# Block-banded first attention group in a TensorE-bound encoder layer: scores per block of 32 positions, one tile per projection unit

## What is computed

```python
ATT_GROUPS = ((128, 1), (512, 4), (2048, 16))   # window, dilation; 8 heads of 64 each
# query at t attends to keys t + j*dil, |j| <= window/(2*dil): group 0 to |offset| <= 64
s = where(mask, q . k, -inf);  m = max(s);  p = exp(s - m);  l = sum(p);  acc = p @ v
# over the three groups: w = exp(m_g - max m);  att = sum(w*acc) / sum(w*l)
```

## Time and profile before

| | |
|---|---|
| median of 3 runs | 2489.22 µs |
| profiled execution, span from first to last instruction | 2486.3 µs |
| PE busy | 2460.4 µs (99%) |
| DVE busy / ACT busy | 1648.8 µs (66%) / 1385.6 µs (56%) |
| granted TensorE clock, mean | 0.996 |

### The profile page before, as it was taken

The page is one execution under the profiler, slowest core; times in us unless marked ns, Lnnn a source line. Parts: engine busy times, 40 slices in busy tenths (PEclk is TensorE's granted clock), DMA queues, the critical chain, the costliest instruction groups (busy, mean ns, idle before and its releaser), DMA issues.

```text
span 2486.3 us, 36774 instructions
## 1 busy us (share of the span) xinstructions
PE 2460.4 (99%) x12848; PEld 2096.6 (84%) x12848; DVE 1648.8 (66%) x2070; ACT 1385.6 (56%) x1542; POOL 323.1 (13%) x287
## 2 busy tenths in 40 slices
PE   8999999999999999999999999999999999999998
PEld 7898989788898989897887688888888888888886
DVE  5454545453544545554434788888888888888887
ACT  4434344432434444445333677777777777777776
POOL 1313122100013122220001100000000000000000
PEclk9999999999999999999999999999999999999999
DMA  4212121122712121112234999999999999999998
GB/s 173 94 41 86 51 93 47 64 85 93 271 54 84 52 93 57 70 53 75 78 145 158 361 386 395 376 399 382 391 383 387 379 386 385 379 389 390 387 383 305
DMA packets 133489, 550.59 MB, mean 221 GB/s; under 512 B 9392, under 2 KB 10032, under 8 KB 125488
## 3 DMA queue, kind: packets, MB, share of 16 engines
q1 hardware_dynamic: 126368, 524.03, 55.4%
q0 software_dynamic: 7056, 25.69, 3.4%
HBM read 528.72 MB, written 20.97 MB: 221 GB/s over the span
## 4 chain that ended last, share of the span: by engine, by line
PE 98%; DVE 1%; DMA 0%; ACT 0%; issue 0%; POOL 0%; SPq 0%; DVEq 0%; ACTq 0%; POOLq 0%
PE bank L1260 42%; PE bank L925 20%; PE bank L970 12%; PE bank L902 7%; PE bank L945 4%; PE bank L986 3%; PE bank L1093 2%; PE bank L1306 2%; PE bank L1054 1%; PE bank L1021 1%; PE bank L1074 1%; PE bank L1034 1%; PE bank L1059 1%; PE bank L1151 1%; PE bank L1109 0%; PE bank L1005 0%
## 5 line engine op out<-in xcount | busy, mean ns | idle before, releaser
L2304 DVE TENSOR_TENSOR m_lo<-m_raw,m_hi 128x2048 fp32r<-128x2048 f32 x380 | 867.4, 2290 | 121.0 <-ACT m_hi L1717 117.6
L1717 ACT ACTIVATE m_hi<-m_raw 128x2048 fp32r<-128x2048 f32 x382 | 733.5, 1921 | 259.9 <-PE bank L1260 256.7
L925 PE MATMUL bank<-w_hi,h_hi 128*128 128x384 f32 (+1 forms) x1024 | 340.9, 333 | 1.7 <-DVE h_lo L2147 0.9
L925 PE MATMUL bank<-w_hi,h_lo 128*128 128x384 f32 (+1 forms) x1024 | 329.9, 322 | 0.0
L925 PE MATMUL bank<-w_lo,h_hi 128*128 128x384 f32 (+1 forms) x1024 | 329.5, 322 | 0.0
L1260 PE MATMUL bank<-m_hi,xs_hi 128*128 128x512 f32 x1032 | 321.0, 392 | 0.0
L1260 PE MATMUL bank<-m_hi,xs_lo 128*128 128x512 f32 x1032 | 317.9, 389 | 0.0
L1260 PE MATMUL bank<-m_lo,xs_hi 128*128 128x512 f32 x1032 | 317.8, 389 | 0.0
L1854 DVE TENSOR_TENSOR w_lo<-w_raw,w_hi 128x1152 fp32r<-128x1152 f32 (+4 forms) x110 | 140.9, 1282 | 212.5 <-ACT w_hi L1380 212.5
L1260 PEld LDWEIGHTS bank<-m_lo,xs_hi 128*128 128x128 f32 x1032 | 193.8, 188 | 40.4
L1260 PEld LDWEIGHTS bank<-m_hi,xs_lo 128*128 128x128 f32 x1032 | 193.8, 188 | 40.3
(11 more groups left out here) (257 smaller groups left out, 3829.9 us busy)
## 6 DMA issues: line engine op xcount, KB each, us to landing
m_raw<-in_w_exp_gate SPq DMA_DIRECT2D x128, 1024.0 KB, 9.3
m_raw<-in_w_exp_up SPq DMA_DIRECT2D x128, 1024.0 KB, 7.0
m_raw<-in_w_exp_down SPq DMA_DIRECT2D x128, 1024.0 KB, 7.6
w_raw<-in_w_b SPq DMA_DIRECT2D x22, 1536.0 KB, 6.7
w_raw<-in_w_a SPq DMA_DIRECT2D x24, 1024.0 KB, 5.1
w_raw<-in_w_c SPq DMA_DIRECT2D x24, 1024.0 KB, 4.7
w_raw<-in_w_d SPq DMA_DIRECT2D x8, 1024.0 KB, 6.0
xt<-in_x SPq DMA_DIRECT2D x8, 512.0 KB, 8.8
```

Of the source, the lines that this page charges most:

```text
L925: last = pe.matmul(ps_proj[:, proj.slot, 0:cols], a[:, c, tokens], v[:, c, :], start=c == n == 0, stop=c == chunks - 1 and n == 2)
L1717: act.activation(m_hi[slot.slot][:, :, :], m_raw[raw.slot][:, :, :], ACT.Copy)\
L2304: dve.tensor_tensor(m_lo[slot.slot][:, :, :], m_raw[raw.slot][:, :, :], m_hi[slot.slot][:, :, :].bitcast(F32), ALU.subtract)\
```

## The change

The three words `S`, `D` become one `S i` for both, `I` is new, and `T`, `U` transpose four blocks each:

```diff
-    order = "P S0 P D0 P P T0 S1 P U0 D1 P P T1 S2 P U1 D2 P P T2 S3 P U2 D3 P"
+    order = "P S0 P S1 P S2 P S3 P P I P P T0 P U0 T1 P U1 T2 P U2 T3 P"
...
-    extra = {0: (("T", 3),), 1: (("U", 3),), 2: (("V",), ("G",)), 3: (("K", 0), ("K", 1)),
+    extra = {0: (("U", 3),), 1: (("V",),), 2: (("G",),), 3: (("K", 0), ("K", 1)),
```

Queries of group 0 are now held by blocks of 32 positions per residue (`by_block`: a tile is 4 residues x 32), and such a tile meets a window of 64 positions x 4 residues, 256 keys (`window_keys`), in place of 512:

```diff
-                            last = pe.matmul(ps_sc[:, a, :], q[head_rows(a), natural(r)], k[head_rows(a), :],
-                                             start=n == 0, stop=n == 2)
+                            pe.matmul(ps_sc[:, a, 0:2 * P], q[head_rows(a), natural(i)], window_keys(k[head_rows(a), :], i),
+                                      start=n == 0, stop=n == 2)
```

```diff
+                elif what == "I":
+
+                    pe.wait_ge(s_same, 1)
+                    all_read(pe, s_sc_free, sc)
+                    pe.wait_ge(s_spread, t["swap"].n(1))
+                    pe.matmul(ps_sc[:, 0, 0:P], same[:, :], spread.rearrange("p (g k s c) -> p (g k s c)"),
+                              start=True, stop=True).then_inc(s_swapped, 1)
...
+                dve.wait_ge(s_exp, t["score"].n())
+                for side in range(2):
+                    own = stats[:, 0, :, 1 - side, :, :].rearrange("p k i a -> p k (i a)")
+                    last = dve.tensor_tensor(spread[:, :, :, side, :], own.unsqueeze(1).to_broadcast([P, NT, 2, 8]),
...
+                dve.wait_ge(s_swapped, t["swap"].n())
...
+                for i in range(NT):
+                    for side, scores in enumerate((near, wide)):
+                        for a in range(2):
+                            last = dve.tensor_scalar(scores[:, i, a, :], scores[:, i, a, :],
+                                                     factor[:, side, i, a:a + 1], None, ALU.mult)
```

`V` has 32 matmuls of 128 columns; the 8 of 512 columns (group 0) are gone. Their values must lie as the windows do, so SP writes `v_a[0]` to memory, waits, and reads it back shifted, between two weight loads:

```diff
-                            pe.matmul(ps_out[head_rows(a), a, :], v_a[0][:, r, head_rows(a)], prob_t[:, a, r, :],
-                                      start=r == 0, stop=False)
+                    for i in range(NT):
+                        for c in range(2):
+                            rows = window(i) // (BLOCK // 2) + 2 * c
+                            for a in range(2):
+                                last = pe.matmul(block_rows(ps_out[head_rows(a), a, :], i), v_shifted[:, rows, head_rows(a)],
+                                                 near[:, i, a, natural(c)], start=False, stop=i == NT - 1 and c == 1)
...
+                sp.wait_ge(s_out, START + t["out"].n())
+                sp.dma_start(v_kept, v_a[0][:, :, :]).then_inc(s_kept, 16)
+                sp.wait_ge(s_kept, t["swap"].n() * 16 + 16)
+                for r in range(RES):
+                    sp.dma_start(v_shifted[BLOCK * r:BLOCK * (r + 1), :, :], kept_rows(r)).then_inc(s_shifted, 16)
```

More of the change, by code:

```diff
@@ L57 @@
 HALVES = ((0, 4), (4, 8))
-PER_HEAD = {"w": 6, "piece": 18, "proj": 20, "first": 1, "pair": 4, "turned": 4, "tr": 26, "sc": 20, "out": 6, "turn": 16, "rope": 16, "ret": 1,
-            "score": 8, "step": 8, "link": 11, "cut": 1}
+PER_HEAD = {"w": 6, "piece": 18, "proj": 20, "first": 1, "pair": 4, "turned": 4, "tr": 22, "sc": 12, "out": 6, "turn": 16, "rope": 16, "ret": 1,
+            "score": 4, "step": 8, "link": 10, "cut": 1, "swap": 1}
 PER_COL = {"w": 4, "piece": 5, "half": 1, "proj": 4 * COLS, "mix": COLS, "hi": COLS}
@@ L578, in _ @@
         def _(sp):
-            t = {"w": Tally(2)}
+            t = some("w", "proj", "out", "swap")
             w = t["w"]
@@ L883, in _ @@
         def _(pe):
-            t = some("w", "proj", "tr", "sc", "out", "rope", "ret", "step", "half", "turned", "cut")
+            t = some("w", "proj", "tr", "sc", "out", "rope", "ret", "step", "half", "turned", "cut", "swap")
             w, proj, tr, sc, outs = t["w"], t["proj"], t["tr"], t["sc"], t["out"]
@@ L1368, in _ @@
         def _(act):
-            t = some("w", "proj", "tr", "sc", "out", "turn", "ret", "score", "mix", "hi", "first", "turned")
+            t = some("w", "proj", "tr", "sc", "out", "turn", "ret", "score", "mix", "hi", "first", "turned", "swap")
             w, proj, tr, sc, outs = t["w"], t["proj"], t["tr"], t["sc"], t["out"]
@@ new lines, in attention_step @@
+                    for side, scores in enumerate((near, wide)):
+                        for a in range(2):
+                            last = act.activation(scores[:, i, a, :], scores[:, i, a, :], ACT.Exp,
+                                                  bias=stats[:, 0, 0, side, i, a:a + 1], scale=DH ** -0.5,
+                                                  accum_out=stats[:, 0, 1, side, i, a:a + 1])
+                    last.then_inc(s_exp, 1)
+                    score.k += 1
+                elif what == "I":
+                    t["swap"].k += 1
+                    act.wait_ge(s_gap, t["swap"].n())
+                    act.activation(share[:, :, :], gap[:, :, :], ACT.Exp).then_inc(s_share, 1)
+                elif what == "T":
+                    act.wait_ge(s_tr, tr.n(1))
+                    act.activation(near[:, arg[0], :, :], ps_tr[:, tr.slot, :].rearrange("p (a n) -> p a n", a=2),
+                                   ACT.Copy).then_inc(s_tr_free[tr.slot], 1)
+                    tr.k += 1
```

260 lines of the change are left out of this document (153 added, 107 removed).

## The result

The changed kernel takes 2504.0 us (median of 4 runs, 2501.9 to 2505.1) against 2488.9 (2486.6 to 2489.6) before, in runs on the same chip: ratio 1.0063, 95% interval 1.0049 to 1.0077. It is slower by 15 us, where I forecast 2463, with 0.89 on faster. The profiled execution has a span of 2500.1 us (2486.3 before).

What follows compares the result with a forecast made beforehand. PE, busy 99% of the span, was taken as the bound: 8 x 3.9 = 31.2 us gained, 5.2 waited, 26.0 net, so span 2460.3 and median 2463 us; range of 8 in 10: 2450 to 2481.

Steps and rivals of the forecast that it cites:

- `I`: Product of 128 columns behind DVE's spread in the head part: 0.2 us of PE waiting per pair, no slack left.
- `S3`: Score products of tile 3 in the head part: no PE wait forecast for the tiles' scores.
- `K`: Third score tile of retention in the tail: PE waits 0.6 us, six times, +3.6 us in all, because `G` starts later.
- PE's own work: PE's instructions in a head pair: 3.9 us less a pair, 31.2 us over 8 pairs.
- The `S` term: Score products, 256-column pairs at 0.18 us instead of 0.23: 12 pairs by 0.05, -0.6 us a pair (0 to -1.4).
- `T` and `U`: Transposes on PE at 0.10 us each, from 48 to 32 a pair: -1.6 us.
- two small spreads (24.3): DVE's last steps before `I`, after `rqk_lo` at 23.85, done at 24.3; PE is ready at 24.4.
- The exponential: ACT's four accumulating activations of 256 columns per tile, 0.37 us each, in a chain step of 4.85 us.
- rival 1: Softmax chain's step about 0.6 us longer, `I` reached 1.8 us late per pair: +14, 2478 us; chance 0.20.
- rival 3: Chain bounds the head part at `I`, PE waits about 5.9 us a pair: 2509 us; break-even 3.5 us; chance 0.07.
- SP's queue: First later load of retention weights, behind `shift_values`, goes about 292, lands about 298.9: hidden with 3.5 us to spare.
- `T0`: First transposes, 5.7 us after `I`; small steps and first two scalings end about 3.5 us after it: 2.2 us spare.

Runs made afterwards that it cites:

- The last kernel: Changed kernel with the second unit's split early, spread ahead of rqk_lo, turn ahead of split, POOL's differences behind the spread, transposes one unit later: 2451.0 us.
- e1: Changed kernel with POOL's two weight differences that fell beside the spread waiting until the product `I` is done: 2479.8 us.
- e4: Changed kernel with the two spreads put ahead of rqk_lo in DVE's queue, POOL's work left in its place: 2465.9 us.
- f4: Changed kernel with early split, spread ahead of rqk_lo, turn ahead of the split, and retention decays `G` one unit earlier: 2455.0 us.
- f2: Changed kernel with the retention turn ahead of the third of the weight split at each unit of the head part: 2464.2 us.
- g1: Changed kernel with whole early split, spread ahead of rqk_lo, turn ahead of split, POOL's differences behind the spread, `G` ahead of its unit's third split: 2475.2 us.

## Why the prediction was wrong

The account, in profiled spans: 2486.3 before, 2500.1 after. The waits of `I`, `S3` and `K` are 42.3 us and the clock costs 15.2, so PE's own work fell by 42.3 + 15.2 - 13.8 = 43.7. The last kernel says nearly the same from the other side: 2449.6 = 2486.3 + 4.8 of waits - 41.5. Against the forecast span of 2460.3 that is 39.8 us too long: 33.8 more at `I`, 4.5 at `S3`, 15.2 of clock, less 1.2 at `K` and less 12.5 of PE's own work.

- **PE's own work: right in kind, priced too low.** 31.2 forecast, 41 to 44 measured. The `S` term was mis-sized: a pair at 0.12 us gives 12 x 0.11 = 1.3 us in place of 0.6, and the eight short products with it take 0.53 and not 0.64. Four transposes take 0.35, so `T` and `U` give 1.9 and not 1.6. The Trainium skill's rule that I weighed ("TensorE: Matmul & The Clock Gate", section "LDWEIGHTS (loading the stationary operand)") gives the time of one load, 107 ns for 128 columns. That the two loads of a pair follow each other, which would hold it at 0.21, was my step, and the 0.12 measured decides against it for these loads of 64 rows. This error helped the kernel but also brought PE to `I` sooner: at 210.95, behind 0.54 of waiting at `S3`, where my times, counted from DVE's start on tile 0 at 191.85, put it at 211.25; so 0.8 us sooner.
- **The step that failed: "two small spreads (24.3)".** I gave them 0.45 us, the price of steps that run alone, and did not ask what POOL does meanwhile. Two instructions took 3.18 us: 2.7 of the 4.4 us. e1 (POOL moved, the spreads as they were) and e4 (the spreads moved, POOL as it was) show the cause from both sides. The Trainium skill, "SBUF — State Buffer", section "Who interferes with whom", says that VectorE and GpSimd share one pair of SBUF ports, which is an exclusive lock, and that a VectorE instruction with two SBUF inputs contends with a GpSimd instruction that reads SBUF, `tensor_reduce` never, `tensor_scalar` if it enters a 2-port mode. The trace agrees, down to the reduction that is not held (0.29 us in e4) and the `TENSOR_SCALAR` that is (0.84 in f4); in which mode that one ran no trace here shows. An estimate by that page: each spread lasts until one of POOL's differences ends, two of them the 3.57 us of POOL's row.
- **The exponential: 0.49 us, not 0.37.** This is a second mis-sized term. My row was a Square in PSUM without a bias operand; these exponentials run in SBUF with one. Four of them make 0.5 us a tile; with the held statistics step of tile 0 (0.49 us and not 0.17) DVE's starts on the tiles lie 5.56, 5.02 and 4.50 apart (191.85, 197.41, 202.43, 206.93) and not 4.85, 4.65 and 4.1. This is rival 1 in kind, 1.5 us in three steps where it had 1.8. With the exponentials of tile 3, 0.5 more, and PE's earlier arrival it gives the 1.6 that e1 leaves at `I`; the 0.56 at `S3` is the chain's too, as f2 shows, which shortens the chain and loses it. No run made the exponential itself shorter. The trace before had its price: the earlier trace rows shows 0.94 for 768 columns with a bias. ACT's copies from SBUF to SBUF give the part of the width: 0.85 for 768 columns and in the head part

```profile
197.55 0.62 ACT L1380 ACTIVATE w_hi<-w_raw 128x512 fp32r<-128x512 f32 x1
```

for 512, so 0.23 for 256, and 0.94 - 2 x 0.23 = 0.48. The Trainium skill's "ScalarE: Activation LUTs", section "What ACT_TABLE_LOAD costs", gives about 280 ns + 0.833 ns a column with a pointer as bias and 186 ns + 0.833 without; an estimate by it is 493 and 399 ns for 256 columns. The trace agrees with 0.49, and with 0.37 nearly.
- **The break-even of rival 3, 3.5 us of waiting a pair.** It left out that waiting isn't only its own length. The clock added 1.9 us to each 4.4. Measured: 5.0 of waiting in the head part, 0.3 at `K` and 1.9 of clock against 5.5 of work saved. Rivals 1 and 3 also count a longer step three times; the masks and exponentials of tile 3 stand before `I` as well, a fourth time, which in rival 3 leaves out 2.0 us a pair, 16 us.
- **`K`, SP's queue, `T0`:** `K` took 0.4 and not 0.6; SP's load went 2 us later than forecast and was in time. `T0` had no wait, as forecast. The factor step's hold took 1.1 us of its slack: the first two scalings end at 219.89, 4.5 us behind `I` where I had 3.5, and 2.9 us before `T0`; 1.6 of these 2.9 come from the slow clock of the two units between.

So the slower case came about in the place that rival 3 named, but by another mechanism, which was in none of my rivals. What stays open: how much of the 0.3 us still waited at `I` in the last kernel can go, and the 2.2 us between the two accounts of PE's own work.

## What to carry to other kernels

In this kernel a small DVE step with its operands in SBUF cost what its row says only while POOL stood still: where a chain is tight, list what POOL does beside every such step, and move POOL's work or the step. Price an activation by a row with the same kind of bias and memory. And a wait of PE of several us costs more than its length, since the clock falls behind it (4.4 us brought 1.9 more); here an order with five things moved by a place or two turned +15 us into -36.

## What the runs showed of the hardware

- A DVE instruction of 16 to 64 columns takes 0.17 to 0.22 us alone and up to 1.8 us when both its operands are in SBUF and POOL's difference (1.8 us for 768 columns) runs; a `TENSOR_SCALAR` of 4 columns from SBUF to SBUF is held alike (0.17 to 0.84). A `TENSOR_REDUCE` (0.29 beside POOL in e4) and instructions with one operand in PSUM (0.28 in e4, 0.42 for a mask step in f4) take what they take alone.
- After 4.3 us without work TensorE was granted 0.69 and 0.74 of its clock in the next two windows of 3 us, which cost 1.6 us there and 1.9 in the mean of eight places. After 2.6 us without work (g1) a window of 3 us that starts 1.2 us behind the wait showed 0.55. Behind a wait of 1.5 us (e1) the products started 0.23 us apart and the window showed 1.00.
- Products of 256 columns with 64 rows, two heads side by side, start 0.12 us apart per pair; 32 short ones with outputs in four runs of 32 columns take the same time as contiguous ones (1.85 us).
